# Fewer gathered rows between the gate products, two low halves more for VectorE, and ten rows earlier

## The chip, the cores and the metric

One core of a Trainium2 chip runs the whole layer in one launch. The metric is the device time of one execution in microseconds, the median of several runs.

## The reference, cut to what matters

The layer has a mixing part (attention over 8 heads and a gated part, both from one input projection) and a retrieval part on top of it. Rows of text below are about the retrieval part and its neighbours.

```python
h2 = rms_norm(x, norm_ffn)
q  = rms_norm((h2 @ w_query).reshape(t, 8, 256)).reshape(t, 8, 2, 128)
s1, s2 = q[:, :, 0] @ sub_keys[0].T, q[:, :, 1] @ sub_keys[1].T
v1, i1 = top_k(s1, 16); v2, i2 = top_k(s2, 16)
top_score, top_pos = top_k(v1[..., :, None] + v2[..., None, :], 16)   # over 256 pairs
expert_idx, gate = i1[...] * 128 + i2[...], softmax(top_score)        # 128 experts a token
act = gelu(einsum('tkd,td->tk', expert_u[expert_idx], h2)) * gate
x = x + einsum('tk,tkd->td', act, expert_v[expert_idx])
```

There are 512 tokens, 16384 experts and 2048 features.

## The kernel before

Tokens are handled in two ways. For the first 128 tokens ("far") and the last 64, the experts that each token picked are fetched: one gather brings one expert row for each of 128 partitions (1 MB), and VectorE does one pass over it. Of 386 such "rows", 128 are of kind u (product of the expert row with the token, line 1302), 128 of kind v (weighted sum into PSUM, line 1312), the rest are the same for the last tokens, and two copies. For the other 320 tokens every expert is multiplied densely on TensorE, and a table of gates (zero where an expert was not picked) selects.

All weights come as 400 pieces of 1 MB in one fixed order. SyncE loads a piece (line 464), ScalarE rounds it into its high half `ring_hi` (line 665), VectorE (line 1075) or GpSimd (line 590) subtracts that from the raw piece and makes the low half `ring_lo`, and TensorE does three products for each block of a piece. Pieces 128 to 143 are the query weights of token tiles 1 to 3; pieces 144 to 215 are 72 pieces of expert u weights that TensorE multiplies ahead, while VectorE picks the top experts of tiles 1 to 3 (pieces 144 to 179) and then while the gates are built (pieces 181 to 210). A piece stands in one of four places in this part, so a piece's load waits until TensorE has used the piece four before it.

The gates: for each group of 4 tokens VectorE makes one-hot rows (`hot_a`, line 1501, `hot_b`, line 1503), TensorE multiplies them (line 1969), and ScalarE copies the result to `gbuf` (line 997). There are 80 groups in 5 batches of 16. `HOT_BATCH` says how many groups go beside each of the six pieces of a batch: 4, 4, 4, 4, 0, 0. After the fourth piece of a batch, `gbuf` (4 MB) is stored to HBM, half of it by SyncE's queue and half by ScalarE's. VectorE runs at most 3 groups ahead of TensorE. ScalarE rounds the piece two ahead of the one in hand before it copies a group, and it doesn't copy the first group of a batch before the store of the one before it has landed.

Everything is ordered by tables. `ROWS_AT[n]` says how many rows VectorE does at piece n. Its loop over the gated pieces is:

```python
for i in range(HOT_FIRST, PRE):
    lo_upto(min(AHEAD + i + 2, DOWN - 1))      # low half of the piece two ahead
    used += HOT_AT[i]
    hots_upto(used + HOT_RING)                 # one-hot rows of the gates
    rows_step(ROWS_AT[AHEAD + i])
```

Within the attention of tiles 1 to 3 (eight heads, n = 0 to 7), VectorE's order is `block_z(n-1)`, `norm_qk(n+3)`, `ATTEND_ROWS[n]` rows, `keep_sp(n+1)`. The rows that are done beside pieces 144 to 179 stand between the steps of the top-k search, after steps 4, 8, 12, 16 and 20 of each tile.

Row buffers: u rows have two buffers during the attention (0 and 1), and three after it; v rows have a fourth, number 3, which holds `h_far` until the last u row is done. GpSimd issues the gathers in the order of the rows (line 618), each when the row before it in its buffer has been used. In GpSimd's program a gather stands where its buffer's row before lies 3 pieces back, so it comes after the low half that GpSimd makes for that piece.

## Time and profile before

| | |
|---|---|
| median of 3 runs | 3003.98 us (3002.12 to 3006.79) |
| profiled execution, its time | 3010.59 us |
| span of the profiled execution | 3008.9 us |
| granted TensorE clock, mean | 0.982 |
| TensorE busy (products) | 2873.1 us (95%) |
| VectorE busy | 2236.0 us (74%) |
| GpSimd busy | 1531.7 us (51%) |
| ScalarE busy | 1187.2 us (39%) |
| DMA | 915.75 MB, mean 304 GB/s |

The span is what the trace covers; the profiled execution's own time is 1.7 us longer. TensorE's products overlap, so its busy time is close to the span also where it isn't at its peak; its idle times and what ended them tell more. Queue q0 carries GpSimd's gathers, q1 SyncE's loads and stores, q10 those of ScalarE.

### The profile page before, as it was taken

What the parts mean: (1) busy time and instruction counts of PE and PEld (TensorE: products, weight loads), DVE (VectorE), ACT (ScalarE), POOL (GpSimd) and SP (SyncE); (2) the same over time, 40 slices, a digit from 0 to 9 for tenths busy, and PEclk for the clock granted to TensorE, in tenths of its full rate; (3) what the DMA queues carried; (4) which work ended last, traced back from release to release, by engine and by line L of the source; (5) the groups of instructions that cost most, each with busy time, mean ns of one, the idle gap of its engine ahead of it and who ended that gap; (6) DMA issues with size and microseconds to landing.
All of it is one profiled execution on the core that took longest, in us unless ns stands there. A gap on an engine that the chain in (4) does not pass through costs nothing.

```text
span 3008.9 us, 43140 instructions
## 1 busy us (share of the span) xinstructions
PE 2873.1 (95%) x17781; PEld 2716.2 (90%) x17781; DVE 2236.0 (74%) x3112; ACT 1187.2 (39%) x1390; POOL 1531.7 (51%) x628
## 2 busy tenths in 40 slices
PE   7899999978989989999899999999999999999998
PEld 6677788856869989999899899999999999999998
DVE  6756577776777789998786577777677777777886
ACT  7755532457233333333333333333333333333331
POOL 0000163321333468872333578788766776766662
PEclk9999999999999999999999999999999999999999
DMA  9637538854796866666788899999999999999996
GB/s 372 258 142 286 215 129 346 331 219 179 302 349 263 321 225 232 235 217 239 295 310 330 321 363 363 358 366 354 360 351 368 397 359 380 363 371 375 347 364 218
DMA packets 183932, 915.75 MB, mean 304 GB/s; under 512 B 16944, under 2 KB 76448, under 8 KB 78272
## 3 DMA queue, kind: packets, MB, share of 16 engines
q1 hardware_dynamic: 115888, 485.79, 43.1%
q0 software_dynamic: 56112, 406.05, 35.5%
q10 hardware_dynamic: 11808, 22.29, 1.9%
q8 instruction: 74, 1.21, 0.2%
q14 instruction: 50, 0.41, 0.0%
HBM read 872.31 MB, written 41.68 MB: 304 GB/s over the span
## 4 chain that ended last, share of the span: by engine, by line
PE 67%; DVE 17%; DMA 8%; ACT 5%; issue 2%; POOL 1%; SPq 0%; DVEq 0%; ACTq 0%
PE ps L1647 11%; PE ps L1995 9%; PE ps L1997 9%; PE ps L1996 9%; PE ps L1927 5%; PE ps L1928 5%; PE ps L1926 5%; PE ps L1911 4%; DVE ring_lo L1075 4%; PE ps L1634 3%; DMA ring_raw<-peer_u 2%; DMA rows<-peer_u_rows,idx_far 2%; DVE rows L1302 2%; PE ps L1969 2%; ACT ring_hi L665 2%
## 5 line engine op out<-in xcount | busy, mean ns | idle before, releaser
L590 POOL TENSOR_TENSOR ring_lo<-ring_raw,ring_hi 128x2048 fp32r<-128x2048 f32 x215 | 1035.2, 4815 | 715.7 <-ACT ring_hi L665 712.8
L665 ACT ACTIVATE ring_hi<-ring_raw 128x2048 fp32r<-128x2048 f32 x400 | 761.4, 1916 | 622.0 <-DMA ring_raw<-peer_u 203.9
L1926 PE MATMUL ps<-bT_hi,ring_hi 128*128 128x320 f32 x2048 | 642.5, 314 | 5.7 <-DVE ring_lo L1075 3.2
L1995 PE MATMUL ps<-a_hi,ring_hi 128*128 128x320 f32 x2048 | 634.7, 310 | 10.9 <-DVE a_lo L1486 4.2
L1927 PE MATMUL ps<-bT_lo,ring_hi 128*128 128x320 f32 x2048 | 635.4, 310 | 0.0
L1928 PE MATMUL ps<-bT_hi,ring_lo 128*128 128x320 f32 x2048 | 635.1, 310 | 0.0
L1996 PE MATMUL ps<-a_lo,ring_hi 128*128 128x320 f32 x2048 | 632.9, 309 | 0.0
L1997 PE MATMUL ps<-a_hi,ring_lo 128*128 128x320 f32 x2048 | 632.8, 309 | 0.0
L1075 DVE TENSOR_TENSOR ring_lo<-ring_raw,ring_hi 128x2048 fp32r<-128x2048 f32 x185 | 446.8, 2431 | 218.6 <-ACT ring_hi L665 218.3
L618 POOL DMA_INDIRECT rows<-peer_u_rows,idx_far x128 | 228.0, 1781 | 446.0 <-DVE z_far L1302 405.5
L1995 PEld LDWEIGHTS ps<-a_hi,ring_hi 128*128 128x128 f32 x2048 | 384.4, 188 | 17.2 <-issue 9.8
L1926 PEld LDWEIGHTS ps<-bT_hi,ring_hi 128*128 128x128 f32 x2048 | 387.4, 189 | 6.2 <-issue 6.1
L1927 PEld LDWEIGHTS ps<-bT_lo,ring_hi 128*128 128x128 f32 x2048 | 387.2, 189 | 0.0
L1928 PEld LDWEIGHTS ps<-bT_hi,ring_lo 128*128 128x128 f32 x2048 | 386.6, 189 | 0.0
L1996 PEld LDWEIGHTS ps<-a_lo,ring_hi 128*128 128x128 f32 x2048 | 384.5, 188 | 0.0
L1997 PEld LDWEIGHTS ps<-a_hi,ring_lo 128*128 128x128 f32 x2048 | 384.4, 188 | 0.0
L1302 DVE CUSTOM_DVE_ANT_0 rows<-rows,h_far 128x2048 f32<-128x2048 f32 x128 | 324.0, 2546 | 59.5 <-DMA rows<-peer_u_rows,idx_far 58.7
L1540 DVE TENSOR_TENSOR yT<-ps,yT 128x320 f32<-128x320 f32 x496 | 232.2, 485 | 167.4 <-PE ps L1997 159.9
L1312 DVE SCALAR_TENSOR_TENSOR ps<-rows,a_far,ps 128x2048 f32<-128x2048 f32 x127 | 298.2, 2348 | 14.9 <-DMA rows<-peer_v_rows,idx_far 13.0
L618 POOL DMA_INDIRECT rows<-peer_v_rows,idx_far x128 | 136.7, 1068 | 170.2 <-DVE ps L1312 111.6
L1647 PE MATMUL ps<-ring_hi,bT_hi 128*128 128x512 f32 x660 | 187.2, 392 | 10.7 <-DVE ring_lo L1075 10.0
L1647 PE MATMUL ps<-ring_lo,bT_hi 128*128 128x512 f32 x660 | 186.1, 390 | 0.0
(297 smaller groups left out, 3697.0 us busy)
## 6 DMA issues: line engine op xcount, KB each, us to landing
ring_raw<-peer_u SPq DMA_DIRECT2D x128, 1024.0 KB
ring_raw<-peer_v SPq DMA_DIRECT2D x128, 1024.0 KB
ring_raw<-w_in SPq DMA_DIRECT2D x80, 1024.0 KB
ring_raw<-w_out SPq DMA_DIRECT2D x32, 1024.0 KB
ring_raw<-w_query SPq DMA_DIRECT2D x32, 1024.0 KB
g_pair<-gates_scratch SPq DMA_DIRECT2D x64, 320.0 KB
gelu_scratch<-ahead ACTq DMA_DIRECT2D x72, 160.0 KB
g_in<-gelu_scratch SPq DMA_DIRECT2D x72, 160.0 KB
```

The costliest lines, as they stand in the source:

```text
L590: pool.tensor_tensor(ring_lo[s][:], ring_raw[s][:], ring_hi[s][:].bitcast(F32), ALU.subtract)\
L618: pool.indirect_dma_start(out=dst[:], out_offset=None, in_=u_rows if kind == "u" else v_rows, in_offset=bass.IndirectOffsetOnAxis(ap=idx_f ...
L665: act.activation(ring_hi[place(n)][:], ring_raw[place(n)][:], ACT.Copy).then_inc(hi_ok[SLOT[n]], 1)
L1075: dve.tensor_tensor(ring_lo[s][:], ring_raw[s][:], ring_hi[s][:].bitcast(F32), ALU.subtract)\
L1302: dve.tensor_tensor_reduce(out=src, in0=src, in1=h_far[:] if kind == "u" else acc, scale=1.0, scalar=0.0, op0=ALU.mult, op1=ALU.add, accum ...
L1647: last = pe.matmul(ps[:, bank + t, :], w[:, k, t * P:(t + 1) * P], m[s][:, cols], start=first, stop=end)
L1926: pe.matmul(dst, hi[:, e], bT_hi[:, k, 0:NEAR], start=(k == 0), stop=False)
L1927: pe.matmul(dst, hi[:, e], bT_lo[:, k, 0:NEAR], start=False, stop=False)
L1928: last = pe.matmul(dst, lo[:, e], bT_hi[:, k, 0:NEAR], start=False, stop=(k == KD - 1))
L1995: pe.matmul(dst, hi[:, col], a_hi[:, par, e, :], start=(e == 0), stop=False)
L1996: pe.matmul(dst, hi[:, col], a_lo[:, par, e, :], start=False, stop=False)
L1997: last = pe.matmul(dst, lo[:, col], a_hi[:, par, e, :], start=False, stop=(e == GROUP - 1))
```

## The change

Four tables change.

```diff
     if AHEAD <= n < DOWN:
-        return (n - AHEAD - HOT_FIRST) % len(HOT_BATCH) < 2
+        return False
...
-ATTEND_ROWS = (2, 2, 2, 2, 2, 2, 2, 0)
+ATTEND_ROWS = (2, 2, 2, 2, 3, 3, 2, 0)
...
-HOT_ROWS = (1, 0, 1, 0, 2, 2)
+HOT_ROWS = (0, 0, 0, 0, 2, 2)
...
     for n in range(OUT_B, AHEAD - 1):
-        ROWS_AT[n] = 0 if n == QUERY_B - 1 else 1 if n == QUERY_B - 2 or n % 4 == 3 and n < QUERY_B else 2
+        ROWS_AT[n] = 0 if n == QUERY_B - 1 else 1 if n == QUERY_B - 2 or n % 4 == 3 and n < QUERY_B else \
+            2 if n < QUERY_B or n % 2 else 3
```

The first is `lo_on_pool(n)`, which says whether GpSimd makes the low half of piece n: from piece 181 to 215 it now makes none, before it made those of 181, 182, 187, 188 and so on to 212, twelve in all, and VectorE makes them now. Beside the gated pieces, 20 rows are left of 30, all at the two pieces of a batch without gates. Beside the query pieces 128 to 142 there are 38 rows for 30 (three at each even piece), and during the attention of tiles 1 to 3 two more, one at head 4 and one at head 5. From piece 144 to 180 VectorE is thereby ten rows further in the list than before, and the lead shrinks by two with each batch of gates. The last u row is done after step 12 of the top-k search of tile 3, where before it was done beside the second batch of gates. After piece 216 all rows stand where they stood. The added line moves all later line numbers by one.

VectorE during the attention, before: from `block_z(3)` to `keep_sp(5)`. `rows_0` and `rows_1` are the two row buffers; the ISA rows are one u row and the read of its sum.

```order
L1370 TENSOR_TENSOR ps<-ps,block_m_163 128x256
L1371 TENSOR_TENSOR ps<-ps,block_m_163 128x128
L1337 TENSOR_TENSOR qk_n_100<-projB_0_95,small_179 128x384
L1337 TENSOR_TENSOR qk_n_100<-projB_1_96,small_179 128x384
L1302 ISA rows_0_149,z_far_177<-rows_0_149,h_far_93 128x2048
L1302 ISA z_far_177 128x1
L1302 ISA rows_1_150,z_far_177<-rows_1_150,h_far_93 128x2048
L1302 ISA z_far_177 128x1
L1359 SCALAR_TENSOR_TENSOR sp_103<-ps,sp_t_102 128x1152
```

The same place now:

```order
L1338 TENSOR_TENSOR qk_n_100<-projB_1_96,small_179 128x384
L1303 ISA rows_0_149,z_far_177<-rows_0_149,h_far_93 128x2048
L1303 ISA z_far_177 128x1
L1303 ISA rows_1_150,z_far_177<-rows_1_150,h_far_93 128x2048
L1303 ISA z_far_177 128x1
L1303 ISA rows_0_149,z_far_177<-rows_0_149,h_far_93 128x2048
L1303 ISA z_far_177 128x1
L1360 SCALAR_TENSOR_TENSOR sp_103<-ps,sp_t_102 128x1152
```

The third row takes the buffer that the first of the same head has just left.

GpSimd during the top-k search of tile 3, before: low halves of pieces 174 to 179 with the gathers between them (the first gather below is of the row after step 20, the next two of rows beside the first gates).

```order
L590 TENSOR_TENSOR ring_lo_2_65<-ring_raw_2_58,ring_hi_2_51 128x2048
L590 TENSOR_TENSOR ring_lo_4_67<-ring_raw_4_60,ring_hi_4_53 128x2048
L618 DMA rows_0_149<-peer_u_rows,idx_far_175 128x2048
L590 TENSOR_TENSOR ring_lo_0_63<-ring_raw_0_56,ring_hi_0_49 128x2048
L590 TENSOR_TENSOR ring_lo_1_64<-ring_raw_1_57,ring_hi_1_50 128x2048
L618 DMA rows_1_150<-peer_u_rows,idx_far_175 128x2048
L590 TENSOR_TENSOR ring_lo_2_65<-ring_raw_2_58,ring_hi_2_51 128x2048
L590 TENSOR_TENSOR ring_lo_4_67<-ring_raw_4_60,ring_hi_4_53 128x2048
L618 DMA rows_2_151<-peer_u_rows,idx_far_175 128x2048
```

The same place now, from the gather of the last u row (buffer 0): eight low halves (pieces 170 to 177), then the gathers of the first v rows.

```order
L619 DMA rows_0_149<-peer_u_rows,idx_far_175 128x2048
L591 TENSOR_TENSOR ring_lo_2_65<-ring_raw_2_58,ring_hi_2_51 128x2048
L591 TENSOR_TENSOR ring_lo_4_67<-ring_raw_4_60,ring_hi_4_53 128x2048
L591 TENSOR_TENSOR ring_lo_0_63<-ring_raw_0_56,ring_hi_0_49 128x2048
L591 TENSOR_TENSOR ring_lo_1_64<-ring_raw_1_57,ring_hi_1_50 128x2048
L591 TENSOR_TENSOR ring_lo_2_65<-ring_raw_2_58,ring_hi_2_51 128x2048
L591 TENSOR_TENSOR ring_lo_4_67<-ring_raw_4_60,ring_hi_4_53 128x2048
L591 TENSOR_TENSOR ring_lo_0_63<-ring_raw_0_56,ring_hi_0_49 128x2048
L591 TENSOR_TENSOR ring_lo_1_64<-ring_raw_1_57,ring_hi_1_50 128x2048
L619 DMA rows_3_152<-peer_v_rows,idx_far_175 128x2048
L619 DMA rows_1_150<-peer_v_rows,idx_far_175 128x2048
L619 DMA rows_2_151<-peer_v_rows,idx_far_175 128x2048
```

The gather of the row that VectorE does after step 16 of tile 3 (now the first v row, into buffer 3) stood after the low half of piece 173, and stands now after that of piece 177.

VectorE between two batches of gates, before: four rows at the two pieces without gates, then the low half of the piece at which the gates go on (its place is 1), then the gates.

```order
L1312 SCALAR_TENSOR_TENSOR ps<-rows_1_150,a_far_178,ps 128x2048
L1312 SCALAR_TENSOR_TENSOR ps<-rows_2_151,a_far_178,ps 128x2048
L1312 SCALAR_TENSOR_TENSOR ps<-rows_3_152,a_far_178,ps 128x2048
L1312 SCALAR_TENSOR_TENSOR ps<-rows_0_149,a_far_178,ps 128x2048
L1075 TENSOR_TENSOR ring_lo_1_64<-ring_raw_1_57,ring_hi_1_50 128x2048
L1501 TENSOR_SCALAR hot_a_140<-iota128_164,selT_173 128x128 x4
L1503 TENSOR_TENSOR hot_b_141<-iota128_164,selT_173 128x512
```

The same place now:

```order
L1076 TENSOR_TENSOR ring_lo_4_67<-ring_raw_4_60,ring_hi_4_53 128x2048
L1313 SCALAR_TENSOR_TENSOR ps<-rows_2_151,a_far_178,ps 128x2048
L1313 SCALAR_TENSOR_TENSOR ps<-rows_0_149,a_far_178,ps 128x2048
L1076 TENSOR_TENSOR ring_lo_0_63<-ring_raw_0_56,ring_hi_0_49 128x2048
L1313 SCALAR_TENSOR_TENSOR ps<-rows_3_152,a_far_178,ps 128x2048
L1313 SCALAR_TENSOR_TENSOR ps<-rows_1_150,a_far_178,ps 128x2048
L1076 TENSOR_TENSOR ring_lo_1_64<-ring_raw_1_57,ring_hi_1_50 128x2048
L1502 TENSOR_SCALAR hot_a_140<-iota128_164,selT_173 128x128 x4
L1504 TENSOR_TENSOR hot_b_141<-iota128_164,selT_173 128x512
```

Two low halves have come between the rows. On GpSimd the two low halves stood ahead of the four gathers that refill the buffers; now nothing but gathers is left there.

## Rows read from the trace of the kernel before

**Rows 1.** The page: its first line, and the group of low halves on GpSimd.

```profile
span 3008.9 us, 43140 instructions
...
L590 POOL TENSOR_TENSOR ring_lo<-ring_raw,ring_hi 128x2048 fp32r<-128x2048 f32 x215 | 1035.2, 4815 | 715.7 <-ACT ring_hi L665 712.8
```

**Rows 2.** TensorE's waits, 905 to 1690 us: waiter, waited for; total, times, longest (us).

```profile
PE ps L1969 <- ACT gbuf L997: 10.2, 2, 9.5
PE ps L1969 <- DVE hot_b L1503: 8.3, 4, 6.5
PE ps L1892 <- DVE sqcB L1437: 5.7, 1, 5.7
```

**Rows 3.** Windows, second gap: stretch, its length, busy time by engine, granted clock, DMA share, GB/s.

```profile
1450.00:1510.00 60.00, 50.47 (x365) 50.24 (x364) 43.70 (x84) 19.52 (x25) 14.72 (x8) 0.91 0.77 305
```

**Rows 4.** Timeline, GpSimd and VectorE, attention, 690 to 720 us: start, us, what [idle before].

```profile
695.07 2.75 POOL L618 DMA_INDIRECT rows<-peer_u_rows,idx_far  x1 [7.55 <-DVE z_far L1302]
698.12 0.93 POOL L618 DMA_INDIRECT rows<-peer_u_rows,idx_far  x1 [0.30 <-issue]
...
700.64 1.36 DVE L1359 SCALAR_TENSOR_TENSOR sp<-ps,sp_t 128x1152 f32<-128x1152 f32 x1 [3.63 <-ACT sp_t L870]
705.59 2.29 DVE L1302 CUSTOM_DVE_ANT_0 rows<-rows,h_far 128x2048 f32<-128x2048 f32 x1 [0.20 <-DMA rows<-peer_u_rows,idx_far]
```

**Rows 5.** Line 1911 (min/median/max ns, first and last start), timeline of GpSimd and VectorE, query pieces.

```profile
L1911 PE MATMUL ps<-bT_hi,ring_hi x256: 334/334/420, 911.1 to 1055.8; 128*128 128x384 f32 x128
...
1006.21 2.79 POOL L618 DMA_INDIRECT rows<-peer_u_rows,idx_far  x1 [5.26 <-DVE z_far L1302]
1037.51 2.75 POOL L618 DMA_INDIRECT rows<-peer_u_rows,idx_far  x1 [2.48 <-DVE z_far L1302]
...
1013.50 2.29 DVE L1302 CUSTOM_DVE_ANT_0 rows<-rows,h_far 128x2048 f32<-128x2048 f32 x1 [0.90 <-DMA rows<-peer_u_rows,idx_far]
1046.87 6.02 DVE L1302 CUSTOM_DVE_ANT_0 rows<-rows,h_far 128x2048 f32<-128x2048 f32 x1 [3.01 <-DMA rows<-peer_u_rows,idx_far]
1058.31 5.55 DVE L1302 CUSTOM_DVE_ANT_0 rows<-rows,h_far 128x2048 f32<-128x2048 f32 x1 [5.41 <-DMA rows<-peer_u_rows,idx_far]
```

**Rows 6.** Timeline, GpSimd, VectorE and TensorE, end of the search of tile 3.

```profile
1293.66 6.39 POOL L590 TENSOR_TENSOR ring_lo<-ring_raw,ring_hi 128x2048 fp32r<-128x2048 f32 x1 [1.97 <-ACT ring_hi L665]
...
1295.58 6.62 DVE L1302 CUSTOM_DVE_ANT_0 rows<-rows,h_far 128x2048 f32<-128x2048 f32 x1
1322.83 1.85 DVE L1265 TENSOR_TENSOR selB<-gate_eB,small 128x128 f32<-128x128 f32 x1
...
1325.83 0.49 PE L1950 MATMUL ps<-ident,selB 128*128 128x128 f32 x3
```

**Rows 7.** Timeline, SyncE, GpSimd and VectorE, third gap between batches (undisturbed).

```profile
1510.73 0.80 SPq L503 DMA_DIRECT2D gates_scratch<-gbuf  x2
...
1524.77 0.95 POOL L618 DMA_INDIRECT rows<-peer_v_rows,idx_far  x1
...
1512.13 9.72 DVE L1312 SCALAR_TENSOR_TENSOR ps<-rows,a_far,ps 128x2048 f32<-128x2048 f32 x4
1530.33 2.29 DVE L1075 TENSOR_TENSOR ring_lo<-ring_raw,ring_hi 128x2048 fp32r<-128x2048 f32 x1 [8.48 <-ACT ring_hi L665]
```

**Rows 8.** Timeline, VectorE in the first gap; GpSimd, SyncE, ScalarE in the second.

```profile
1401.42 2.29 DVE L1302 CUSTOM_DVE_ANT_0 rows<-rows,h_far 128x2048 f32<-128x2048 f32 x1 [10.86 <-DMA rows<-peer_u_rows,idx_far]
...
1435.96 2.75 POOL L618 DMA_INDIRECT rows<-peer_v_rows,idx_far  x1 [37.36 <-DVE z_far L1302]
...
1442.97 1.06 SPq L503 DMA_DIRECT2D gates_scratch<-gbuf  x2
...
1470.43 1.91 ACT L665 ACTIVATE ring_hi<-ring_raw 128x2048 fp32r<-128x2048 f32 x1 [7.57 <-DMA ring_raw<-peer_u]
```

**Rows 9.** DMA queue q0, 1443 to 1450 us, then 1510 to 1530: packets, MB, share.

```profile
q0 software_dynamic: 186, 1.38, 56.8%
...
q0 software_dynamic: 48, 0.26, 3.1%
```

## Prediction

> **What bounds the kernel now.** The page gives a span of 3008.9 us [rows 1]; the profiled execution took 3010.59 us, which is 6.6 us above the median of the runs, so I make the sum in its frame and carry only the difference over to 3003.98. TensorE is 95% busy, so I went first to its waits between the query pieces and the end of the pieces multiplied ahead. They are few: 10.2 us for ScalarE's copies to `gbuf` (9.5 in one piece), 8.3 us for VectorE's `hot_b` (6.5 in one piece), 5.7 us for VectorE's last squares of the query [rows 2]. 
>
> Then I read the four places that get something new, each with the engine that ends its chain: the attention, the query pieces, the search of tile 3, and the gaps between batches.
>
> **Attention: two rows more, +5 us.** A u row takes 2.29 us, and VectorE waits 3.63 us before `keep_sp(5)` [rows 4], so a third row at head 4 looks free. It isn't, for it needs the buffer that the first row of this head just left. The refill of that buffer starts at 695.07 [rows 4]. What a refill takes is seen on the next one: started at 698.12, its row could start at 705.59, 7.5 us later [rows 4]. With 7 us for the first, the third row runs from 702.1 to 704.4, and `keep_sp(5)` starts there and not at 700.64: +3.7. At head 5 the third row waits for a refill again, started after a first row that is itself late by 3.7; I put 1.3 on it, an estimate. This chain (`keep_sp`, TensorE, `block_z`, ScalarE, scores of the next head) is what the heads wait for, each for the one before, so it all shows: +5. Bounds: 2.3 (a refill 1.5 us quicker) and 7.
>
> **Query: eight rows more, +7 us.** 16 pieces go from 911.1 to about 1056 us, 9.1 us a piece [rows 5]. 38 rows need one each 3.6 us. Three buffers in a ring allow one each third of a turn: refill plus row plus 0.35 us to GpSimd's start. A refill takes 7.3 us (1006.21 to 1013.50) to 9.4 us (1037.51 to 1046.87) [rows 5], so a turn takes 9.9 to 12.0 us, a row 3.3 to 4.0. At the quick end the ring keeps up; at the slow end 35 rows lose 0.38 us each, 13 us. And the eight gathers of 1 MB more make refills no quicker. On top, at piece 142 there is one row more at the end of the chain: before, its second row came late (its refill stands on GpSimd behind the low half of piece 144) and started at 1058.31 for 5.55 us [rows 5]; only after it VectorE adds the squares for which TensorE waits [rows 2]. One row more behind it is 2.3 us. Bounds: 2.3 and 15; I take 7, as the low halves for TensorE are still a few us early and swallow part of the lag.
>
> **Search of tile 3: the first v row, +5 us.** VectorE is busy without a gap there, and TensorE reaches the transposes that need its result just when it is ready: result at 1322.83 + 1.85 = 1324.7, transposes at 1325.83 [rows 6]. The row after step 16 started at 1295.58 [rows 6]. It is now the first v row, in the buffer that only the last u row frees, and its gather stands behind the low half of piece 177. That one started at 1293.66, waiting for ScalarE's high half [rows 6], so it can't be earlier. It took 6.39 us beside VectorE's row, which took 6.62 instead of 2.29: they held each other up. If VectorE waits, GpSimd needs 4.8 us (the mean of all its low halves [rows 1]), so the gather starts at about 1298.5, the row at 1306.5 with 8 us of refill, and ends at 1308.8; before it ended at 1302.2. That is 6.6 us late, less 1.15 us of slack: +5. Bounds: 1 (refill of 4 us, and contention saved at later steps) and 8.
>
> The Trainium skill, page "SBUF — State Buffer", section "SBUF: two separate sides", says that a VectorE instruction with two inputs in SBUF and a GpSimd instruction shut each other out for a whole instruction. Rows 6 agree. By that rule, taking the twelve low halves from GpSimd gives VectorE back up to 4.3 us for each that fell on such an instruction; but the v rows read PSUM, and TensorE doesn't wait for VectorE inside a batch, so by this rule too the sum stays.
>
> **Gates: two low halves for two rows, +12 us.** For VectorE the batch is the same: two low halves of 2.2 us come, two rows of about 2.3 go. The order at the gap counts. Before, in an undisturbed gap, the gates' store starts at 1510.73 (call it 0). VectorE does four rows in a burst, then waits for the piece at which the gates go on; its low half starts at +19.6, behind 1.9 us of ScalarE [rows 7, 8]. GpSimd is held by two low halves until +14.0 and gathers only then [rows 7], so the store and this piece have the DMA for themselves: between 1510 and 1530 the gathers' queue moved 0.26 MB, 3.1% [rows 9]. This gap cost TensorE 0.5 us: there is no slack in it. Now GpSimd has nothing but gathers. The rows end at about +8, +10, +15 and +17, each gather starts at once, and 2 to 4 MB fall in front of the piece. The second gap of before shows what that does: four gathers from 1435.96, the store at 1442.97, and the high half of that piece at 1470.43, so +27.5 and not +17.7 [rows 8]. The gathers' queue had 57% of the DMA then, 1.38 MB in 7 us [rows 9], or 0.2 MB/us. That gap cost the 9.5 us of rows 2. All queues together move 305 GB/s at a share of 0.77, so 0.40 MB/us when full [rows 3]. With 0.2 of it taken from +9.5 on, the piece is in when 0.4(T - 17.7) = 0.2(T - 9.5): T = 25.9, 8.2 us late. With 0.15 it is 22.6, 4.9 us late; as late as in the second gap is 9.8. TensorE is late with it, in each of four gaps. I take 6.1, nearer to the low end, as the third and fourth gather come piecemeal: 4 x (6.1 + 0.5 + 1.7) = 33 us, against 21.4 now: +12. Bounds: 4 x (4.9 + 0.5 + 1.7) - 21.4 = +7 and 4 x (9.8 + 0.5 + 1.7) - 21.4 = +27; without any harm from the gathers it would be 4 x 0.5 - 21.4 = -19.
>
> What is surely removed is the wait of the first gap (VectorE stood 10.86 us for a row whose gather was behind the two low halves on GpSimd [rows 8]) and the burst before the second store.
>
> The Trainium skill, page "DMA: Bandwidth & Descriptors", section "Queues, rings and completion order", says that each DMA engine takes turns between its queues, packet by packet. With three queues at work that would leave the gathers a third, some 0.13 MB/us, and the gap's delay just below the lower bound, near 4.1 us (+4 in the sum instead of +12); rows 9 show more than a third.
>
> **Sum.** 5 + 7 + 5 + 12 = 29 us, so 3010.6 + 29 = 3039.6 in the profile's frame, and a median of 3004 + 29 = 3033 us. The last gap and all behind it I leave at zero: the same rows stand there, and TensorE bounds that part.
>
> **Rivals.**
> - The gathers don't hold the piece up (the store ends first anyway), and the gaps run clean: -19 beside the gates. For it speaks that the load is ahead of them in time; against it the second gap. With the attention, query and search at their lower bounds (2.3 + 2.3 + 1 = 5.6) it is 13 us faster, 2991; with the forecast's 17 it comes to 3002, no change. It decides if less than 0.5 MB of gathers lands before that piece; the point of balance, with my 17 us elsewhere, is a gap of about 0.6 us. 10% faster, 6% no change.
> - The gathers take everything they can: all 4 MB in front, the query ring at its slow end. 27 + 13 + 5 + 7 = 52, 3056 us. 12%.
> - The gates as forecast, but refills quick (7 us or less) everywhere: 2.3 + 2.3 + 1 and 7 to 12 for the gates, 13 to 18 in all, 3017 to 3022 us. 17%.
> - The forecast, 3022 to 3046: 50%. The remaining 5% is no change by the low ends together (gap delays of 3 us, 3 us elsewhere).
>
> **Numbers.** No measurement here tells less than 0.2% (6 us) from no change. Slower: 50 + 17 + 12 = 79, and I round to 0.80; no change 0.10, faster 0.10. The range leaves out the faster rival and the upper part of the slow one: 3008 to 3050.
>
> **What would show it.** Right: TensorE waits of 5 to 10 us for `gbuf` or `hot_b` once in each of four gaps, the high half there at +22 to +27 from the store; VectorE waiting for row DMAs two or three times in the attention, and `keep_sp(6)` later by 5; a VectorE wait before the row of step 16 of tile 3; TensorE's wait for the last squares above 8 us. Wrong: gaps without a wait, or a q0 share near nothing in the 18 us after a store. The forecast would be most wrong if the rows at the gap came later than I have them, behind the high halves, so that their gathers fall behind the piece.

## The result and the profile after

The changed kernel takes 3017.08 us (median of 9 runs, 3008.77 to 3026.21), the kernel before 3006.79 us beside it (9 runs, 3002.12 to 3014.02). The ratio is 1.0037, with an interval of 1.0022 to 1.0052: slower by 11 us (7 to 16). The forecast was slower by 29 us. The direction was right, the size wrong, and the direction was in part luck: the gates, forecast to add 12 us, gave 12 back.

The page of the changed kernel: its first line, the engines' busy times, GpSimd's low halves. To be compared with [rows 1]; the twelve low halves are gone from GpSimd (203 for 215), and the span is 13.0 us longer.

```profile
span 3021.9 us, 43141 instructions
...
PE 2875.0 (95%) x17781; PEld 2719.8 (90%) x17781; DVE 2225.8 (74%) x3124; ACT 1191.3 (39%) x1392; POOL 1463.1 (48%) x616
...
L591 POOL TENSOR_TENSOR ring_lo<-ring_raw,ring_hi 128x2048 fp32r<-128x2048 f32 x203 | 974.8, 4802 | 695.5 <-ACT ring_hi L666 693.5
```

To see where the time went I read the first and last start of six kinds of products, by line, in both kernels. First the kernel before: attention values, squares of the query, pieces multiplied ahead, the turns of the search's result, gates, down part.

```profile
L1828 PE MATMUL ps<-projB,w_att x96: 275/275/275, 666.7 to 737.3; 128*128 128x128 f32 x96
L1892 PE MATMUL ps<-neg,sqcB x48: 169/250/373, 963.8 to 1067.2; 128*128 128x1 f32 x48
L1926 PE MATMUL ps<-bT_hi,ring_hi x2048: 302/309/628, 1070.1 to 2954.6; 128*128 128x320 f32 x187
L1950 PE MATMUL ps<-ident,selB x9: 270/272/273, 1156.2 to 1326.0; 128*128 128x128 f32 x9
L1969 PE MATMUL ps<-hot_a,hot_b x640: 270/275/583, 1334.9 to 1625.9; 128*128 128x128 f32 x160
L1995 PE MATMUL ps<-a_hi,ring_hi x2048: 302/309/419, 1682.7 to 2997.6; 128*128 128x320 f32 x187
```

The same lines of the changed kernel, one number higher.

```profile
L1829 PE MATMUL ps<-projB,w_att x96: 275/275/276, 671.9 to 746.1; 128*128 128x128 f32 x96
L1893 PE MATMUL ps<-neg,sqcB x48: 169/250/370, 970.6 to 1088.4; 128*128 128x1 f32 x48
L1927 PE MATMUL ps<-bT_hi,ring_hi x2048: 302/309/629, 1092.7 to 2967.6; 128*128 128x320 f32 x187
L1951 PE MATMUL ps<-ident,selB x9: 270/273/475, 1179.1 to 1355.1; 128*128 128x128 f32 x9
L1970 PE MATMUL ps<-hot_a,hot_b x640: 270/275/551, 1366.0 to 1644.6; 128*128 128x128 f32 x160
L1996 PE MATMUL ps<-a_hi,ring_hi x2048: 303/309/419, 1701.3 to 3010.6; 128*128 128x320 f32 x187
```

Differences of these starts give a table of stretches (attention: first to last value; query: to the last squares; search: first piece ahead to the last turn; gates: first to last gate product; down: first to last down product).

| us | before | after | difference |
|---|---|---|---|
| start of the attention values | 666.7 | 671.9 | +5.2 |
| attention | 70.6 | 74.2 | +3.6 |
| query | 329.9 | 342.3 | +12.4 |
| to the first piece ahead | 2.9 | 4.3 | +1.4 |
| search | 255.9 | 262.4 | +6.5 |
| to the first gate product | 8.9 | 10.9 | +2.0 |
| gates | 291.0 | 278.6 | -12.4 |
| down | 1314.9 | 1309.3 | -5.6 |

Two rows are no effect of the change. The attention values start between 664.1 and 674.2 us in the sixteen profiles of this study, though nothing differs ahead of them; and the down part took 1309.1 to 1316.9 us in the kernels with as many rows left for it as before. So +5.2 and -5.6 are what one execution differs from another, and they cancel. What is left is that the early rows cost 25.9 us up to the first gate product, and that the gates then give 12.4 back. I had forecast that the gates cost 12.

TensorE's waits, 905 to 1700 us of the changed kernel (waiter, waited for; total, times, longest), to be held against [rows 2]:

```profile
...
PE ps L1893 <- DVE sqcB L1438: 10.4, 1, 10.4
PE ps L1912 <- DVE ring_lo L1076: 7.2, 3, 4.3
PE ps L1970 <- ACT gbuf L998: 7.0, 4, 3.8
PE ps L1951 <- DVE selB L1266: 5.8, 1, 5.8
PE ps L1927 <- DVE small L1458: 3.9, 1, 3.9
```

The two long waits of before in the gates (9.5 and 6.5 us) are gone; in their place each of the four gaps has a short one, 7.0 us in all. Three waits are new or longer ahead of the gates: the low halves of the query pieces, the last squares, the result of the search.

### The profile page after: what moved, and what is told of

Read it like the earlier page. It is cut to its first block, busy times and chain, and to the rows that moved or that the text cites. A ratio compares the mean times of both kernels' runs of the same rounds, so it can differ in the third digit from the quotient of the medians.

```text
span 3021.9 us, 43141 instructions
## 1 busy us (share of the span) xinstructions
PE 2875.0 (95%) x17781; PEld 2719.8 (90%) x17781; DVE 2225.8 (74%) x3124; ACT 1191.3 (39%) x1392; POOL 1463.1 (48%) x616
## 4 chain that ended last, share of the span: by engine, by line
PE 75%; DMA 11%; DVE 7%; ACT 4%; POOL 1%; issue 1%; SPq 0%; DVEq 0%; ACTq 0%
PE ps L1648 13%; PE ps L1996 10%; PE ps L1998 9%; PE ps L1997 9%; PE ps L1927 8%; PE ps L1929 8%; PE ps L1928 8%; DMA rows<-peer_u_rows,idx_far 4%; PE ps L1635 3%; DMA ring_raw<-peer_u 3%; DVE ring_lo L1076 2%; PE ps L1970 2%; DVE rows L1303 2%; ACT ring_hi L666 2%; DMA ring_raw<-w_in 1%; PE ps L1622 1%
## 5 line engine op out<-in xcount | busy, mean ns | idle before, releaser
L591 POOL TENSOR_TENSOR ring_lo<-ring_raw,ring_hi 128x2048 fp32r<-128x2048 f32 x203 | 974.8, 4802 | 695.5 <-ACT ring_hi L666 693.5
L1076 DVE TENSOR_TENSOR ring_lo<-ring_raw,ring_hi 128x2048 fp32r<-128x2048 f32 x197 | 456.2, 2331 | 214.8 <-ACT ring_hi L666 214.6
L1303 DVE CUSTOM_DVE_ANT_0 rows<-rows,h_far 128x2048 f32<-128x2048 f32 x128 | 313.5, 2463 | 80.6 <-DMA rows<-peer_u_rows,idx_far 79.9
L1648 PE MATMUL ps<-ring_hi,bT_hi 128*128 128x512 f32 x660 | 187.7, 393 | 10.6 <-DVE ring_lo L1076 9.9
L1648 PE MATMUL ps<-ring_hi,bT_lo 128*128 128x512 f32 x660 | 186.5, 391 | 0.0
```

What stands on the lines that cost most here:

```text
L591: pool.tensor_tensor(ring_lo[s][:], ring_raw[s][:], ring_hi[s][:].bitcast(F32), ALU.subtract)\
L1076: dve.tensor_tensor(ring_lo[s][:], ring_raw[s][:], ring_hi[s][:].bitcast(F32), ALU.subtract)\
L1303: dve.tensor_tensor_reduce(out=src, in0=src, in1=h_far[:] if kind == "u" else acc, scale=1.0, scalar=0.0, op0=ALU.mult, op1=ALU.add, accum ...
L1648: last = pe.matmul(ps[:, bank + t, :], w[:, k, t * P:(t + 1) * P], m[s][:, cols], start=first, stop=end)
```

## The experiments

All kernels were timed in several rounds against the kernel before on the same chip. The total tells 0.15 to 0.2% at best, 5 us; most verdicts below rest on the stretches, which tell more, because a stretch under equal tables varies less: the attention by 1 to 4 us, the search and the gates by up to 3, the down part by 8. The query stretch is the loosest, 4 us without the early rows and 9 with them.

### One part of the change at a time

**Gates alone.** Attention and query rows as before; the ten rows fall to the last part.

```diff
-ATTEND_ROWS = (2, 2, 2, 2, 3, 3, 2, 0)
+ATTEND_ROWS = (2, 2, 2, 2, 2, 2, 2, 0)
...
-            2 if n < QUERY_B or n % 2 else 3
+            2
```

> Only the gates' part of the change (fewer rows beside the gated pieces, all low halves there on VectorE); attention and query rows as before, so the ten rows go to the pieces after the down part's first half. My theory: the gates' part wins by itself what the traces show, 12 us between the first and the last gate product, and the ten late rows cost at most 2 us where TensorE bounds: 10 to 12 us faster than before (ratio 0.996 to 0.9967), the first gate product within 2 us of before's. Rival: the 12 us are not a gain of this part, the changed kernel only caught up what it had lost before the gates; then this kernel is within 3 us of before, and waits of 9 and 6 us for gbuf and hot_b are still there.

Ratio 1.0021 (0.9999 to 1.0042): not faster, my theory fell. The gates' stretch is 287.7 us (1333.0 to 1620.7), only 3.3 less than before, with 14.2 us of waits for hot_b and gbuf in it; and the ten late rows cost 12 us and not 2 (down stretch 1326.9 us). VectorE still waits for a row in a gap, and now in two of them; its timeline:

```profile
1396.56 2.29 DVE L1303 CUSTOM_DVE_ANT_0 rows<-rows,h_far 128x2048 f32<-128x2048 f32 x1 [7.50 <-DMA rows<-peer_u_rows,idx_far]
...
1461.81 2.29 DVE L1303 CUSTOM_DVE_ANT_0 rows<-rows,h_far 128x2048 f32<-128x2048 f32 x1 [8.28 <-DMA rows<-peer_u_rows,idx_far]
```

Both are the fourth u row of a gap. GpSimd makes no low half there, so it isn't held; the row waits because u rows have three buffers, and a gap has four rows.

**Early rows alone.** Ten rows early, the gates' tables of before.

```diff
-        return False
+        return (n - AHEAD - HOT_FIRST) % len(HOT_BATCH) < 2
...
-HOT_ROWS = (0, 0, 0, 0, 2, 2)
+HOT_ROWS = (1, 0, 1, 0, 2, 2)
```

> Only the ten early rows (attention and query), gates as before. My theory: first gate product 31 us later than before (4 to 9 in the attention, 16 in the query, 6 in the search), the gates part as long as before, and some 5 us given back after it: 20 to 26 us slower than before (ratio 1.0067 to 1.0087). Rival (catching up): the gates part gets shorter here too, by about 12 us, and the kernel is only 10 to 13 us slower, as the changed kernel.

Ratio 1.0064 (1.0041 to 1.0088), 19 us. The rival's mechanism was right, and my theory of an unchanged gates' stretch wrong: with the gates' tables untouched the stretch fell from 291.0 to 271.6 us. Its total was not right: the search took 266.2 us, 4 more than in the changed kernel. The line of the gates:

```profile
L1970 PE MATMUL ps<-hot_a,hot_b x640: 270/275/377, 1358.1 to 1629.7; 128*128 128x128 f32 x160
```

In its second gap SyncE's store, GpSimd's first gather and ScalarE's high half of the piece behind the store stand at 0, +14.0 and +17.0:

```profile
1457.82 1.23 SPq L504 DMA_DIRECT2D gates_scratch<-gbuf  x2
...
1471.86 0.95 POOL L619 DMA_INDIRECT rows<-peer_v_rows,idx_far  x1 [0.15 <-issue]
...
1474.86 1.91 ACT L666 ACTIVATE ring_hi<-ring_raw 128x2048 fp32r<-128x2048 f32 x1 [3.15 <-DMA ring_raw<-peer_u]
```

That is the undisturbed gap of [rows 7], in all four gaps now.

**Low halves alone**, no early rows.

```diff
     if AHEAD <= n < DOWN:
-        return (n - AHEAD - HOT_FIRST) % len(HOT_BATCH) < 2
+        return False
```

> Only the twelve low halves moved from GpSimd to VectorE; thirty rows beside the gates and all else as before. Theory that the rows are what counts: VectorE has 4.4 us more in each batch and still the rows beside the third batch piece, so its waits ahead of hot_b stay or grow; within 4 us of before, up or down. Rival, that GpSimd's low halves ahead of the gathers were what counted (the 10.86 us wait in the first gap): 8 to 12 us faster.

Ratio 1.0016 (0.9999 to 1.0033), stretch 295.7 us: as the theory had it, and not 8 to 12 us faster. Its second gap is the worst of all. All four v gathers stand ahead of the store at 1436.34, the first by 7 us, and the high half comes 30.5 us after it:

```profile
1429.33 2.75 POOL L619 DMA_INDIRECT rows<-peer_v_rows,idx_far  x1 [39.42 <-DVE z_far L1303]
...
1466.80 1.91 ACT L666 ACTIVATE ring_hi<-ring_raw 128x2048 fp32r<-128x2048 f32 x1 [10.97 <-DMA ring_raw<-peer_u]
```

**Rows alone**, no early rows.

```diff
-HOT_ROWS = (1, 0, 1, 0, 2, 2)
+HOT_ROWS = (0, 0, 0, 0, 2, 2)
```

> Only the ten rows taken from beside the gates (they go to the late part); GpSimd makes its twelve low halves as before. Theory that the rows are what counts: 10 to 12 us faster than before, and since two low halves still hold GpSimd until about 14 us after the gates' store, gap delays are at most as in the changed kernel (1 to 4 us of wait in each gap). Rival, that the low halves on GpSimd are what counted: within 4 us of before, with VectorE waits of over 8 us for rows at the gaps.

Ratio 1.0027 (1.0006 to 1.0048): a miss. The stretch is 285.9 us, 5 less than before; in the first two gaps VectorE waits 11.1 and 11.5 us for the fourth u row, and the ten rows that fall to the last part cost 15 us there (down stretch 1330.3). So neither half of the gates' edit is what shortened the stretch by itself.

**Eight early rows, old gates.** As the kernel with early rows alone, without the two attention rows.

> Eight query rows early, attention and gates as before. The kernel with all ten early rows and the gates as before had a gates' stretch of 271.6 us, against 291.0 before and 278.6 changed, so what shortened it was that the last u row comes before the gates (after it there are four row buffers, and no four gathers at once before the second store), and not the edit of the gates. My theory: with eight rows early that still holds: stretch 270 to 274 us, attention as before, query and search 15 to 25 us later: 0 to 8 us slower than before (ratio 1.000 to 1.0027), and 3 to 8 us faster than the changed kernel. Rival: the gates' edit is what shortened it and the 271.6 were chance: stretch 285 us or more, 15 us or more slower than before (ratio over 1.005).

The stretch is 269.6 us, as the theory said; the total, ratio 1.0048 (1.0030 to 1.0065), is more than it gave. The down stretch was 1321.8 us. Of this 8.6 us is one wait of TensorE, by GpSimd's and TensorE's timelines:

```profile
2299.88 2.29 POOL L626 DMA_INDIRECT rows<-peer_u_rows,idx  x1 [8.94 <-DMA y<-rows]
2302.19 4.50 POOL L591 TENSOR_TENSOR ring_lo<-ring_raw,ring_hi 128x2048 fp32r<-128x2048 f32 x1
...
2306.75 0.64 PE L1927 MATMUL ps<-bT_hi,ring_hi 128*128 128x320 f32 x1 [8.61 <-POOL ring_lo L591]
```

The low half stands behind a gather, and the gather waits until the result of the far tokens has been stored from its buffer. GpSimd waits there in all kernels (8.7 us before, 8.3 changed), but how soon TensorE needs the next low half differs with where the rows fall: it waited 4.8 to 5.6 us for that low half in the three kernels with eight or ten rows more left for this part, and 3 us or less in all others.

**No attention rows**, otherwise as changed.

```diff
-ATTEND_ROWS = (2, 2, 2, 2, 3, 3, 2, 0)
+ATTEND_ROWS = (2, 2, 2, 2, 2, 2, 2, 0)
```

> The changed kernel without the two attention rows; the eight query rows stay, so the last u row still is done before the gates, after step 20 of the search of tile 3. My theory: 4 us less in the attention than the changed kernel, the gates' stretch (first to last gate product) stays short, 277 to 281 us as there: 3 to 5 us faster than the changed kernel (ratio to before 1.002 to 1.0027). Rival: the attention rows are hidden, and the first gap gets a wait for the first v rows: no gain or up to 5 us slower than the changed kernel.

Ratio 1.0032 (1.0014 to 1.0050), 1.5 us below the changed kernel's and inside its interval. The attention stretch was 66.8 us. Over sixteen profiles it is 69.2 us in the mean of the eight without the two rows (66.8 to 70.6), and 74.5 in the mean of the eight with them (73.4 to 74.8): +5.3 us. The gates' stretch stayed at 278.5 us. The mechanism was as forecast, the total doesn't resolve it: 3 to 5 us were expected, 1.5 us was found.

**No query rows**, otherwise as changed: six u rows are left for the gates.

```diff
-            2 if n < QUERY_B or n % 2 else 3
+            2
```

> The changed kernel without the eight query rows (the two attention rows stay). Six u rows are left when the gates begin. My theory: the query stretch goes back to 326 to 330 us (from 342), the search to 256 (from 262), but the u rows reach into the first two gaps again, four in the first where only three buffers serve them, so the gates' stretch grows from 278.6 to 285 to 290 us, and eight rows more fall to the last part (up to 10 us there). In all within 8 us of the changed kernel, ratio to before 1.000 to 1.004. Rival: the gates' edit keeps the gates' stretch at 279 us or less by itself; then this kernel is 15 us or more faster than the changed one (ratio 0.999 or less).

Ratio 1.0049 (1.0036 to 1.0062), a little above the expected 1.000 to 1.004, and by the expected stretches: query 329.3 us, search 256.9, gates 290.0, down 1323.4. The rival (gates at 279 us or less by their edit alone) is out. The first gap, with four u rows, cost TensorE 4.8 us for `hot_b`. The second, with two u and two v rows, cost more, 9.8 us, and I had not foreseen how: VectorE stood 11.7 us ahead of the first v row.

```profile
1476.77 2.35 DVE L1311 TENSOR_SCALAR ps<-rows,a_far 128x2048 f32<-128x2048 f32 x1 [11.67 <-issue]
```

The profile names no releaser; but GpSimd issued that row's gather only at +10.2 us, when the last u row was done (1463.07 against 1462.72), so I put the wait down to it. The switch itself costs when it falls into a gap.

### What the u rows do in the gaps

The stretch falls when the last u row comes ahead of the gates. If that is the cause, the kernel before can be mended with no row moved to another stage: never more than three u rows in a gap, and the last u row one piece earlier, so that its followers' gathers are not under way at the second store.

```diff
-HOT_ROWS = (1, 0, 1, 0, 2, 2)
+HOT_ROWS = (1, 1, 1, 0, 2, 1) + (1, 1, 0, 0, 2, 2) + 3 * (1, 0, 1, 0, 2, 2)
```

> The kernel before, with only the rows of the first two batches of gates placed in another way, six each as before: 1,1,1,0,2,1 in the first (three rows in the gap, as many as u rows have buffers) and 1,1,0,0,2,2 in the second (the last u row one piece earlier, so the four gathers of the v rows no longer stand just ahead of the second store). No row moves to another stage. My theory: the 10.86 us wait for a row in the first gap and the delay of the piece in the second gap go, 15 to 20 us of the 21.4 us that the gates lose before: stretch 271 to 278 us, ratio to before 0.9935 to 0.996. Rival: one row more between the gates makes VectorE late with the one-hot rows, or the gathers of the last u rows hit the first piece behind the store in the same way: stretch still 285 us or more, ratio over 0.998.

Ratio 0.9943 (0.9923 to 0.9964): 17 us faster than before, and 28 faster than the changed kernel by the two ratios. The stretch is 279.5 us, 1.5 us above the expected range; its fall of 11.5 us is most of the gain, and the rest is within what the total and the other stretches vary. A second kernel moves the last u row one piece more ahead.

```diff
-HOT_ROWS = (1, 0, 1, 0, 2, 2)
+HOT_ROWS = (2, 1, 1, 0, 2, 1) + (1, 0, 0, 0, 2, 2) + 3 * (1, 0, 1, 0, 2, 2)
```

> The kernel before with rows 2,1,1,0,2,1 beside the first batch and 1,0,0,0,2,2 beside the second: the last u row one piece earlier than in the kernel that was 0.57% faster than before (its gates' stretch 279.5 us, of which the second gap still lost 3 us to gathers that were under way at the store: 0.79 MB in the ten us behind it). My theory: those gathers have landed by the store, the second gap's high half goes from +20.5 to about +18, stretch 275 to 278 us, ratio to before 0.992 to 0.995. Rival: two rows at the first gated piece make the one-hot rows late, and what the second gap gives the first batch takes: stretch 280 us or more.

Ratio 0.9952 (0.9933 to 0.9970), stretch 276.9 us, high half in the second gap at +16.6 (in the one before at +20.5). The gap is clean, as expected; in total the two can't be told apart. The gates' line and the waits for them, 905 to 1700 us, in this kernel:

```profile
L1969 PE MATMUL ps<-hot_a,hot_b x640: 270/275/453, 1334.8 to 1611.7; 128*128 128x128 f32 x160
```

```profile
PE ps L1969 <- DVE hot_b L1503: 4.7, 5, 2.3
...
PE ps L1969 <- ACT gbuf L997: 1.0, 2, 0.5
```

Against [rows 2], 18.5 us of waits have become 5.7. Both kernels beat the one before and the changed one.

### What the changed gates cost

With early rows, so with v rows alone in the gaps, the stretch was 271.6 and 269.6 us with the old gates, and 276.4 to 279.1 us in five kernels with the new ones. The next kernels ask what makes these 7 us.

**Low halves back on GpSimd**, all else as changed.

```diff
-        return False
+        return (n - AHEAD - HOT_FIRST) % len(HOT_BATCH) < 2
```

> The changed kernel with the twelve low halves given back to GpSimd (the twenty rows beside the gates and the ten early rows stay). With v rows alone in the gaps the gates' stretch was 276 to 279 us in five kernels with the changed gates, and 270 to 272 in two with the old. The open question is which half of the gates' edit makes these 7 us. My theory: the free GpSimd, since its gathers then stand at +8 us from the store and not at +14; given the low halves back the stretch is 269 to 272 us, the high half behind the store at +16.5 to +18.5 in all four gaps, TensorE's waits for gbuf and hot_b 3 us or less. Rival: the two low halves on VectorE, or the rows, make VectorE late: the stretch stays at 276 us or more if it is the rows.

Ratio 1.0030 (1.0015 to 1.0045). The stretch is 269.5 us, and GpSimd's first gather stands at +14.0 in each gap, the high half at +17.2 to +18.5: the free GpSimd made the 7 us, not the rows.

```profile
L1970 PE MATMUL ps<-hot_a,hot_b x640: 270/275/378, 1362.0 to 1631.5; 128*128 128x128 f32 x160
```

But what it gave back in the gates it took in the search, whose stretch was 266.5 us. With piece 181's low half on GpSimd, VectorE's last product pass of the search ran beside it; GpSimd's and VectorE's timelines of this kernel:

```profile
1332.17 11.22 POOL L591 TENSOR_TENSOR ring_lo<-ring_raw,ring_hi 128x2048 fp32r<-128x2048 f32 x2
...
1339.01 6.53 DVE L1258 TENSOR_TENSOR eqB<-eqB,i12fB 128x2048 f32<-128x2048 f32 x1
```

and the same pass in the changed kernel, where GpSimd was idle:

```profile
1346.81 2.29 DVE L1258 TENSOR_TENSOR eqB<-eqB,i12fB 128x2048 f32<-128x2048 f32 x1
```

4.2 us, right ahead of the result for which TensorE waits (10.1 us for it here, 5.8 in the changed kernel; 10.0 with early rows alone). The Trainium skill, page "SBUF — State Buffer", section "SBUF: two separate sides", has this rule, that an instruction of VectorE with two inputs in SBUF and one of GpSimd shut each other out, and this trace agrees (6.53 us for 2.29). I had weighed the rule at the low halves between the gates and found that it changed nothing. It did at one that falls into the search.

**Gathers a little earlier**: all four rows at the fifth piece.

```diff
-HOT_ROWS = (0, 0, 0, 0, 2, 2)
+HOT_ROWS = (0, 0, 0, 0, 4, 0)
```

> The changed kernel with all four rows of a batch at the fifth piece instead of two at the fifth and two at the sixth, so GpSimd issues the four gathers at about +5, +7, +10 and +12 us from the gates' store and not at +8, +10.5, +15 and +17.5. The step that failed is the size of the delay a gather puts on the piece behind the store. My theory now: while three queues are at work the gathers get about 27% of the DMA, 0.11 MB/us, so some 0.4 to 0.6 MB more land before the piece: its high half moves from +19.2 to about +20.5, TensorE waits 1 to 2 us more in each of four gaps, 4 to 8 us in all against the changed kernel (ratio to before 1.005 to 1.0065). Rival (what the prediction took): gathers take half or more, 0.2 MB/us, so 1 MB more lands and the high half is at +22 to +24: 12 to 20 us more than the changed kernel (ratio 1.008 to 1.010).

A miss for both: ratio 1.0037 (1.0022 to 1.0053), stretch 276.4 us, no longer than in the changed kernel. The gathers didn't come as early as I wrote: the first two stood at +8.1 and +10.5 as there (VectorE makes the low half first), only the last two came 2 us earlier. Queue q0 moved 1.03 to 1.06 MB from +10 to +20, for 1.08 to 1.17 in the changed kernel.

**Gathers clearly earlier**: two of the four rows one piece ahead.

```diff
-HOT_ROWS = (0, 0, 0, 0, 2, 2)
+HOT_ROWS = (0, 0, 0, 2, 2, 0)
```

> The changed kernel with the rows 0,0,0,2,2,0 beside each batch and not 0,0,0,0,2,2: two gathers then stand just ahead of the gates' store (about -2 and 0 us) and two behind it (+8 and +10). What it asks: is it the place ahead of the store that makes gathers costly (the high half was at +27.5 before and +30.5 in the kernel with only low halves moved, both with four gathers from -7 on), or their number? My theory: the place. Two gathers ahead of the store run at half of the DMA or more while the store's queues start, 1.5 MB or more land in the first 10 us, and the high half comes at +21 to +25, so TensorE waits 3 to 7 us in each gap: stretch 288 to 300 us, 10 to 20 us slower than the changed kernel. Rival: three queues share evenly from the start, the high half is at +19 to +21 as in the changed kernel, stretch under 284 us.

Ratio 1.0093 (1.0073 to 1.0113). The stretch of 292.4 us and the high half at +21.8 to +22.9 are as my theory had them, but not for its reason: no gather stood ahead of the store. They stood at +3.6, +6.1, +10.5 and +13.0, as SyncE's, GpSimd's and ScalarE's timelines in the third gap show:

```profile
1530.86 0.80 SPq L504 DMA_DIRECT2D gates_scratch<-gbuf  x2
...
1534.49 0.94 POOL L619 DMA_INDIRECT rows<-peer_v_rows,idx_far  x1 [50.02 <-DVE ps L1313]
1536.94 2.74 POOL L619 DMA_INDIRECT rows<-peer_v_rows,idx_far  x1 [1.52 <-DVE ps L1313]
...
1552.68 1.91 ACT L666 ACTIVATE ring_hi<-ring_raw 128x2048 fp32r<-128x2048 f32 x1 [6.69 <-DMA ring_raw<-peer_u]
```

So a place ahead of the store isn't needed for harm; by the four gaps in the table below, what counts is how much of the gathers lands before the piece. The rows of queue q0 (packets, MB, share) from +10 to +20 of the third gap, first with the low halves back on GpSimd, then in the changed kernel, then here:

```profile
q0 software_dynamic: 38, 0.31, 7.4%
```

```profile
q0 software_dynamic: 154, 1.15, 27.1%
```

```profile
q0 software_dynamic: 205, 1.55, 36.8%
```

| kernel, gap | first gather | q0, 0 to +20, MB | high half | gates' stretch |
|---|---|---|---|---|
| low halves on GpSimd, third | +14.0 | 0.31 | +18.1 | 269.5 |
| changed, third | +8.1 | 1.15 | +19.4 | 278.6 |
| rows one piece ahead, third | +3.6 | 1.74 | +21.8 | 292.4 |
| before, second | -7.0 | 3.07 | +27.5 | 291.0 |

From the first row of the table, the piece is later by 1.3 us for the first 0.84 MB more (1.5 us a MB), by 2.6 us a MB up to the third row and 3.4 us a MB up to the last. At the full rate of 0.4 MB/us [rows 3] one MB is worth 2.5 us. (In the last row one gap of four is of this kind; its 291.0 us hold the wait in the first gap too.)

### The other terms

**No row at the end of the query chain**: the third row of piece 142 is done at piece 129.

```diff
-            2 if n < QUERY_B or n % 2 else 3
+            3 if n == QUERY_B + 1 or QUERY_B <= n < AHEAD - 2 and n % 2 == 0 else 2
```

> The changed kernel with the third row of piece 142, the last query piece with rows, done at piece 129. Tests how much of the query's loss (12 us in the stretch, 14 with the step to the ahead pieces) is the one row at the chain's end. Forecast for it 2.3 us, the rest is the ring. My theory: TensorE's wait for the last squares falls from 10.4 to 7 to 8 us, the query stretch by 2 to 3 us; VectorE's backlog is the ring's, so it doesn't fall to the 5.7 us of before. Rival: there is no backlog, the end row is all: wait at 6 us or less, stretch 332 us or less.

Ratio 1.0030 (1.0014 to 1.0046). TensorE's wait for the last squares fell from 10.4 to 5.7 us, all of the way to before's, as the rival had it; in the seven other kernels with eight early query rows it is 9.6 to 10.6 us, so this is no chance. The stretch fell only to 338.5 us and not to the rival's 332; these stretches vary from 337.6 to 346.9 us, so its fall can't be told from nothing. So the end row is 4.7 us. That the ring is the rest was not tested by itself; for it speaks that VectorE waits 31.9 us for u rows between 905 and 1100 us in the changed kernel, 28.7 here, 12.5 before.

**Gathers of the first v rows earlier** in GpSimd's program, by one low half or two.

```diff
-    return 2 if n >= DOWN else ROW_LAG
+    return 2 if n >= DOWN else 1 if AHEAD + 30 <= n < AHEAD + 35 else ROW_LAG
```

> The changed kernel with the gathers of the first three v rows two low halves earlier in GpSimd's program (and one each for the ones beside them). Tests the term for the search of tile 3, forecast +5, seen as 262 us against 256 before. My theory (the row after step 16 waits for a gather that stands behind the low half of piece 177): the search stretch falls back to 256 to 258 us and TensorE's wait of 5.8 us for the search's result goes to 1 us or less. Rival: the gather then waits on GpSimd for h_far's buffer, the low halves behind it come late, and TensorE waits for them: stretch 262 us or more. Either way the total moves by no more than 6 us.

Between the two: TensorE's wait for the search went from 5.8 to 2.7 us, the stretch from 262.4 to 260.1 (kernels with the rows of before: 255.9 to 257.1). The total doesn't show it, ratio 1.0037 (1.0023 to 1.0051). The gather then waits 3.25 us for the last u row itself, whose buffer it needs, so the low half was half of the reason.

## Why the prediction was wrong in size

**Attention, forecast +5: right.** VectorE starts the third row of head 4 only after 5.31 us of waiting for its refill; GpSimd's and VectorE's timelines after, to hold against [rows 4]:

```profile
699.94 2.75 POOL L619 DMA_INDIRECT rows<-peer_u_rows,idx_far  x1 [7.56 <-DVE z_far L1303]
...
707.19 2.29 DVE L1303 CUSTOM_DVE_ANT_0 rows<-rows,h_far 128x2048 f32<-128x2048 f32 x1 [5.31 <-DMA rows<-peer_u_rows,idx_far]
709.40 1.35 DVE L1360 SCALAR_TENSOR_TENSOR sp<-ps,sp_t 128x1152 f32<-128x1152 f32 x1
```

The refill took 7.2 us (707.19 - 699.94). Counted from the first attention value, `keep_sp(5)` is at 37.5 and not 33.9 us: +3.6, where the forecast's working has +3.7. The mean over the profiles is +5.3.

**Query, forecast +7: too small.** In the mean of eight profiles with the eight rows as changed the stretch is 340.9 us (337.6 to 346.9), in seven with none 327.6 (326.0 to 329.9): +13.3, within the bounds of 2.3 to 15 but at their slow end. I had taken the middle on the ground that the low halves are some us early. They aren't early enough: TensorE waits 7.2 us for `ring_lo` of query pieces, where it never waited before. The end row was taken at 2.3 us and is 4.7: its refill is the last in a queue of late ones, as VectorE's timeline shows.

```profile
1080.23 2.53 DVE L1303 CUSTOM_DVE_ANT_0 rows<-rows,h_far 128x2048 f32<-128x2048 f32 x1 [4.95 <-DMA rows<-peer_u_rows,idx_far]
```

**Search, forecast +5: right.** +6.5 here, and 262.2 to 262.6 us in four kernels with these tables. VectorE waits 5.96 us for the first v row, whose gather stands behind GpSimd's low half of piece 177. The mechanism is the one named; GpSimd needed 6.40 us for that low half and not the 4.8 I had hoped for.

```profile
1316.50 6.40 POOL L591 TENSOR_TENSOR ring_lo<-ring_raw,ring_hi 128x2048 fp32r<-128x2048 f32 x1 [1.97 <-ACT ring_hi L666]
1323.05 0.95 POOL L619 DMA_INDIRECT rows<-peer_v_rows,idx_far  x1 [0.15 <-issue]
...
1328.91 2.35 DVE L1311 TENSOR_SCALAR ps<-rows,a_far 128x2048 f32<-128x2048 f32 x1 [5.96 <-DMA rows<-peer_v_rows,idx_far]
```

**Gates, forecast +12, found -12: the step that failed.** Its first half, that the gates lose 21.4 us before and that this is all there is to win, was right: with v rows alone in the gaps and GpSimd's low halves kept they take 270.2 us (mean of three kernels), 20.8 less than 291.0. Its second half, "4 x (6.1 + 0.5 + 1.7) = 33 us" for the changed gaps, is the term that was mis-sized. It measured 278.0 - 270.2 = 7.8 us (278.0 is the mean of five kernels with no low halves on GpSimd in the gates). The third gap of the changed kernel, by SyncE, GpSimd, ScalarE and VectorE:

```profile
1523.83 0.80 SPq L504 DMA_DIRECT2D gates_scratch<-gbuf  x2
...
1531.91 0.94 POOL L619 DMA_INDIRECT rows<-peer_v_rows,idx_far  x1 [47.40 <-DVE ps L1313]
...
1543.27 1.91 ACT L666 ACTIVATE ring_hi<-ring_raw 128x2048 fp32r<-128x2048 f32 x1 [5.55 <-DMA ring_raw<-peer_u]
...
1545.22 2.29 DVE L1076 TENSOR_TENSOR ring_lo<-ring_raw,ring_hi 128x2048 fp32r<-128x2048 f32 x1 [4.20 <-ACT ring_hi L666]
```

The order and the times of the gathers came out as foreseen (+8, +10.5, +15, +17.5). The rate did not. I took 0.2 MB/us from [rows 9], a stretch at whose start four gathers already were under way and the store was just beginning. With three queues at work the gathers got 0.115 MB/us (1.15 MB in 10 us, 27.1% of the DMA). My own formula with this rate gives 0.4(T - 17.7) = 0.115(T - 9.5), T = 21.0, a delay of 3.3 us; measured were +19.2, +18.2, +19.4 and +21.7, 1.9 us late in the mean. What makes 1.9 of 3.3 stays open. The 1.7 us for a slow clock came in one gap of four. TensorE stood 1.2, 0.5, 1.5 and 3.8 us for `gbuf` in the four gaps; around the third wait the granted clock stayed at 1.00, behind the fourth it fell to 0.83 in the mean of 20 us, a mix of the two levels, and the first products took 0.47 us for 0.31. The windows around the third and the fourth (length, busy times, granted clock, DMA share, GB/s):

```profile
1543.80:1563.80 20.00, 18.00 (x135) 17.50 (x134) 17.52 (x42) 9.88 (x13) 0.00 (x0) 1.00 0.75 301
...
1605.00:1625.00 20.00, 17.96 (x118) 18.00 (x119) 17.20 (x42) 8.42 (x12) 0.00 (x0) 0.83 0.60 226
```

That is at most 0.17 x 20 = 3.4 us, an estimate, for 4 x 1.7 = 6.8 in the forecast. Over all gates the clock was 0.99, against 0.97 before.

The Trainium skill, page "DMA: Bandwidth & Descriptors", section "Queues, rings and completion order", says that the DMA engines take turns between queues packet by packet. Its third for each of three queues is near the 27.1, 41.0 and 32.5% measured here. I set it aside because rows 9 showed 57%; by it the delay was 4.1 us, still twice the measured one.

The rival "clean gaps" had 10% and 6%. It was nearest in the gates, -19 where -13 was found, though not by its condition: it wanted less than 0.5 MB of gathers ahead of the piece, and 1.08 to 1.17 MB came. The rival with quick refills, 17%, was nearest in the total (13 to 18 us), and that is luck: it has the gates at +7 to +12 and the query at +2.3. What I had not seen at all is why the early rows and the gates belong together: they end the u rows ahead of the gates. I had both waits of before down as things to be removed (the fourth row in the first gap, the burst ahead of the second store), but ascribed their going to the gates' edit. That is the second half of the failed step. The kernels with early rows alone show them gone without it, the ones with the gates' edit alone show most of them still there.

**Everything behind the gates, forecast 0: right** for what the profiles can tell, -5.6 in the one pair, 1309 to 1317 us over the kernels with the same rows there. The down part took 1317.4 and 1321.8 us in the two kernels with the old gates and fewer rows left for it. In the second, 8.6 us is the one wait shown above; in the first, TensorE's waits for low halves sum to 11.2 us, none over 2.8 (5.6 us before). Nothing was tried for either.

**The sum.** By the means of the stretches: 5.3 + 13.3 + 1.4 + 6.0 (search) + 2.0 - 13.0 (gates, 278.0 for 291.0) = 15 us, at the upper edge of the timed 7 to 16 us. Ahead of the gates this is 28 us where I had 17: 6.3 us is the query, and 3.4 us (the steps of 1.4 and 2.0 on the two sides of the search) stood in no term. At the gates it is 25 us less than I had. The two errors have opposite signs and partly cancel, so the total looks better than its terms.

## What to carry to other kernels

When a list of work has two kinds with different buffer counts, look where the switch from one to the other falls: here the rows on its two sides cost 21 us, and placing them anew within two batches made the kernel 0.5% faster, where moving ten of them across three stages made it slower. A queue's share read in one stretch holds only for the queues that were at work there; before taking it as a rate elsewhere, count who is active in each half of the stretch. And an edit that frees an engine also frees what this engine issues next: GpSimd's low halves were what kept four gathers away from the piece behind the store. The same edit can act both ways: the low half of the one piece that falls into the search was better on VectorE.

## What was not expected of the hardware

A gather of 1 MB issued at +8 us from a store of 4 MB moved nothing before +10. Queue q0 then got 23 to 28% of the DMA from +10 to +20 (five kernels), with the store's two queues still at work, and 85 to 92% from +20 to +28 in the kernels whose gathers began at +14, when the store was through. And two passes of VectorE over the same 128x2048 elements differ in what GpSimd does to them: a u row beside GpSimd's low half took 6.6 us for 2.29 [rows 6], four v rows in a row beside two low halves 9.7 us for 4 x 2.35 [rows 7], which is hardly slower. The v row reads and writes PSUM; that this is the reason was not tested.
